# Weight sums of the 19 panel pairs: from VectorE into background transfers that add in device memory

## The reference, cut to what matters

```python
def _sq_relu_mlp(h, w1, w2):
    return jnp.square(jax.nn.relu(h @ w1)) @ w2
...
    h = _layer_norm_2(ALPHA * h + 0.5 * _swiglu(h, ffn2_w_gate[l], ffn2_w_up[l], ffn2_w_down[l]),
```

## Time and profile before

| | |
|---|---|
| median of 3 runs | 2706.53 us (2704.66 to 2708.64) |
| span of the profiled execution, first to last instruction | 2704.5 us |
| TensorE busy | 2652.7 us (98%) |
| VectorE busy | 1448.8 us (54%) |
| ScalarE busy | 1080.8 us (40%) |
| GpSimd busy | 279.4 us (10%) |
| DMA | 233 MB, 86 GB/s over the span |
| mean granted TensorE clock | 0.992 of full speed |

### The profile page before, as it was taken

One profiled execution on the slowest core, in us unless ns is written; L12 is line 12 of the kernel. 1 busy time (PEld: TensorE's weight loads), 2 busy tenths in 40 slices (PEclk: granted clock), 3 DMA queues, 4 the chain that ended last, 5 costly groups with the idle time before them and its releaser, 6 DMA issues.

```text
span 2704.5 us, 39939 instructions
## 1 busy us (share of the span) xinstructions
PE 2652.7 (98%) x16572; PEld 2343.7 (87%) x16572; DVE 1448.8 (54%) x2445; ACT 1080.8 (40%) x1743; POOL 279.4 (10%) x350
## 2 busy tenths in 40 slices
PE   8999999999999999999999999999999999999997
PEld 7888999999988888888888988888888897988887
DVE  5664665545543434576546543435666664645554
ACT  4655443323433233353234422323566543533333
POOL 1000300001200000210000300002211130300002
PEclk9999999999999999999999999999999999999998
DMA  4111223223111212222234232222322222222321
GB/s 143 55 48 48 79 94 127 86 79 126 55 63 63 97 62 85 86 86 94 76 104 141 85 113 97 86 94 71 110 86 71 70 87 79 66 98 82 106 88 61
DMA packets 67685, 232.98 MB, mean 86 GB/s; under 512 B 9008, under 2 KB 11440, under 8 KB 67120
## 3 DMA queue, kind: packets, MB, share of 16 engines
q1 hardware_dynamic: 67504, 230.41, 25.9%
HBM read 228.25 MB, written 2.10 MB: 85 GB/s over the span
## 4 chain that ended last, share of the span: by engine, by line
PE 88%; DVE 4%; ACT 3%; POOL 2%; issue 2%; DMA 1%; SPq 0%; DVEq 0%; POOLq 0%; ACTq 0%
PE ps L683 70%; PE ps L725 7%; PE ps L1030 2%; POOL R L3075 1%; PE ps L1161 1%; PE ps L733 1%; PE ps L925 1%; PE ps L885 1%; PE ps L1016 1%; POOL S L3060 1%; ACT HT L1450 1%; DVE R L2211 1%; DVE HT L2204 1%; DVE LENT L2162 1%; PE ps L1237 1%
## 5 line engine op out<-in xcount | busy, mean ns | idle before, releaser
L683 PE MATMUL ps<-XH,WH 128*128 128x264 f32 (+2 forms) x1552 | 470.5, 341 | 10.1 <-DVE XL L3034 7.6
L683 PE MATMUL ps<-XL,WH 128*128 128x264 f32 (+2 forms) x1552 | 457.1, 332 | 0.0
L683 PE MATMUL ps<-XH,WL 128*128 128x264 f32 (+2 forms) x1552 | 456.1, 332 | 0.0
L683 PE MATMUL ps<-HH,LENT 128*128 128x264 f32 (+2 forms) x2000 | 444.3, 318 | 3.0 <-DVE LENT L2162 1.9
L683 PE MATMUL ps<-XH,LENT 128*128 128x264 f32 (+2 forms) x1808 | 436.8, 332 | 5.0 <-DVE XL L2228 4.8
L2162 DVE TENSOR_TENSOR WL<-RAW,WH 128x1024 fp32r<-128x1024 f32 (+2 forms) x260 | 316.0, 1218 | 222.3 <-ACT WH L1406 221.0
L1406 ACT ACTIVATE WH<-RAW 128x1024 fp32r<-128x1024 f32 (+2 forms) x260 | 267.9, 1034 | 228.3 <-PE ps L683 187.6
L683 PEld LDWEIGHTS ps<-HH,LENT 128*128 128x128 f32 x2000 | 324.3, 189 | 31.6 <-DVE LENT L2162 2.3
L683 PEld LDWEIGHTS ps<-XH,LENT 128*128 128x128 f32 x1808 | 302.1, 189 | 42.5 <-DVE XL L2228 5.6
L2162 DVE TENSOR_TENSOR LENT<-RAW,LENT 128x1024 fp32r<-128x1024 f32 (+2 forms) x202 | 245.2, 1222 | 140.4 <-ACT LENT L1406 139.9
L683 PEld LDWEIGHTS ps<-XH,WH 128*128 128x128 f32 x1552 | 270.5, 190 | 50.0 <-issue 18.2
(11 more groups left out here) (256 smaller groups left out, 3395.4 us busy)
## 6 DMA issues: line engine op xcount, KB each, us to landing
RAW<-in_wf SPq DMA_DIRECT2D x128, 512.0 KB, 3.3
RAW<-in_wr SPq DMA_DIRECT2D x48, 512.0 KB, 3.3
RAW<-in_wg SPq DMA_DIRECT2D x44, 512.0 KB, 3.3
RAW<-in_wu SPq DMA_DIRECT2D x44, 512.0 KB, 3.3
RAW<-in_wd SPq DMA_DIRECT2D x32, 512.0 KB, 3.3
RAW<-in_we SPq DMA_DIRECT2D x24, 512.0 KB, 3.4
RAW<-in_wm SPq DMA_DIRECT2D x24, 512.0 KB, 3.2
RAW<-in_wro SPq DMA_DIRECT2D x16, 512.0 KB, 3.2
```

What stands on the lines that cost most here:

```text
L683: mm = e.matmul(o[:, to:to + m], wt, xt[:, k, c0 + a * m:c0 + (a + 1) * m], start=(n == 0 and j == 0), stop=(n == nk - 1 and j == 2))
```

## The change

The four sums of each pair are no longer made on VectorE. GpSimd issues, for seven groups of pairs (three for each MLP with two pairs each, one for the gates with seven), four copies from the weight matrix into a new array in device memory (`WSUM`) and then four transfers that add to what is there (`accum_op=ALU.add`): S1 = b2 + b1, S3 = a1 + b1, S2 = a1 + S1, S4 = a2 + S2. [...] Copies and adds are issued at fixed places of GpSimd's program: for the first MLP right after the constants, for the second after the first normalization (copies) and in the retention heads (adds), for the gates after `ln10` (copies), `ln11` (S1, S3), the memory normalization (S2) and `ln1` (S4). Each add waits for its copy, S2 and S4 also for the sum before.

SP loads by split, not by panel: `first` 512 KB, `22` 256 KB, `S13` and `S24` 512 KB each, the last two from `WSUM`, after the semaphores of their adds. A `RAW` buffer is free again once its one split is done. `S13` comes before `S24`, and `pair_steps` offers a split after each of the seven products. The new function `pair_up` has no pairs to work on here (no `wu` panel is in `PAIR_FIRST`).

```diff
-            if end:
-                s = ring.popleft()
...
+            s = ring.popleft()
+            ring.append(s)
+            units.append((kind, i, s, had.get(s)))
+            had[s] = (i, end)
...
-PAIR_UNITS = (("first", 2), ("22", 5), ("sums", 0), ("gap", 0), ("S24", 6), ("S13", 7))
+PAIR_UNITS = (("first", 2), ("22", 5), ("S13", 7), ("S24", 6))
...
-                if n in (1, 3, 5, 7):
-                    self.upto(i + 8, 1)
+                self.upto(i + 8, 1)
...
-        def weight_sums(i):
...
-                    e.tensor_tensor(b2, b2, acc(("pair", i, "A"), 1)[:, 0:n].unsqueeze(1).broadcast_to([P, 2, n]),
-                                    ALU.add).then_inc(*S.pair_add(i, "second"))
+                    e.scalar_tensor_tensor(b2, b2, -1.0, acc(("pair", i, "A"), 1)[:, 0:n].unsqueeze(1).broadcast_to([P, 2, n]),
+                                           ALU.mult, ALU.subtract).then_inc(*S.pair_add(i, "second"))
...
+        def sum_copies(key):
+
+            (name, first), n = key, SUM_PAIRS[key]
+            w4 = A[name][first:first + SUM_STEP[name] * n].rearrange("(q a) p (h k) c -> a h p q (k c)", a=SUM_STEP[name], h=2)
+            to = WSUM[key].rearrange("q p s c -> s p q c")
+            for m, (a, h) in {"S1": (1, 1), "S3": (0, 0), "S2": (0, 0), "S4": (0, 1)}.items():
+                e.dma_start(to[SUM_AT[m]], w4[a, h]).then_inc(*S.sum_copy(key, m))
+
+        def sum_add(key, m):
...
+            w.wait_ge(*S.sum_copy[key, m])
+            if m == "S2":
+                w.wait_ge(*S.sum_add[key, "S1"])
+            if m == "S4":
+                w.wait_ge(*S.sum_add[key, "S2"])
+            more = {"S1": w4[1, 0], "S3": w4[1, 0], "S2": to[SUM_AT["S1"]], "S4": to[SUM_AT["S2"]]}[m]
+            e.dma_start(to[SUM_AT[m]], more, accum_op=ALU.add).then_inc(*S.sum_add(key, m))
...
+        for key in ff_sums[0]:
+            sum_copies(key)
+        sum_adds(ff_sums[0], "S1", "S3", "S2", "S4")
         down_norm("ln00")
+        for key in ff_sums[1]:
+            sum_copies(key)
         down_norm("ln01")
         for h in range(4):
+            sum_adds(ff_sums[1], *(("S1", "S3"), ("S2",), ("S4",), ())[h])
...
         down_norm("ln10")
+        for key in gu_sums:
+            sum_copies(key)
         down_norm("ln11")
+        sum_adds(gu_sums, "S1", "S3")
...
+        sum_adds(gu_sums, "S2")
         down_norm("ln1")
+        sum_adds(gu_sums, "S4")
...
+            else:
+                key, q = SUM_OF[i]
+                for m in {"S13": ("S1", "S3"), "S24": ("S2", "S4")}[kind]:
+                    w.wait_ge(*S.sum_add[key, m])
+                a = SUM_AT[{"S13": "S3", "S24": "S2"}[kind]]
+                src = WSUM[key][q][:, a:a + 2, :].rearrange("p s n -> p (s n)")
+            if u >= NRAW:
+                w.wait_ge(*S.w_lo[u - NRAW])
+            e.dma_start(RAW[:, u % NRAW, 0:unit_cols(u)], src).then_inc(*S.raw_in(u))
```

More of the change, by code:

```diff
@@ L238, in lent_until @@
 def lent_until(name, idx, end=NSCR):
-    return max((i, 7 if i in PAIRS else 9) for _, i, s, _ in UNITS if i < AT[name, idx] and s and s[0] == "lent" and s[1] < end)
+    return max((i, 7 if i in PAIRS else 9) for _, i, s, _ in UNITS if i < AT[name, idx] and s[0] == "lent" and s[1] < end)
 class Signal:
@@ L1387, in split @@
             kind, i, place, before = UNITS[u]
[L1388 to L1401, removed]
+            raw, n = RAW[:, u % NRAW, :], unit_cols(u)
+            w.wait_ge(*S.raw_in[u])
             if before is not None:
@@ L1479, in relu2, with pair @@
             e.activation(HH[:, j, c0:c0 + T], TMP[:, j % 4, 0:T], ACT.Square).then_inc(*S.h_hi(stage, j, half))
-        def pair(i, rows, take):
+        def pair(i, tiles, take):
             stage = PAIRS[i]
             n = T_HALF[stage]
-            a, b = (TMP[:, r, :] for r in rows)
+            a, b = tiles
             to = {"11": (a, "A", 0), "S1": (b, "B", n), "S2": (a, "A", n), "22": (b, "D", 0)}
@@ L1501, in take @@
                 relu_free(i + 1, None)
-            pair(i, (idx % 4, idx % 4 + 1), take)
+            pair(i, [TMP[:, j % 4, :] for j in (idx, idx + 1)], take)
             for j in (idx, idx + 1):
@@ L1518, in pair_gate, with pair_up, take @@
                 e.activation(t, t, ACT.Silu).then_inc(*S.silu(i + n, None))
+        def pair_up(name, idx):
+            i, stage = AT[name, idx], f"gu{name[2]}c{idx // 8}"
+            def take():
+                if (name, idx - 2) in PAIR_FIRST:
+                    w.wait_ge(*S.up[AT[name, idx - 1], None])
+            pair(i, WIDE, take)
+            for j in (idx, idx + 1):
+                w.wait_ge(*S.up[AT[name, j], None])
+                w.wait_ge(*H_free(stage))
+                to_h(stage, j % 8, None, TMP[:, j % 4, 0:512], NM, 512)
         def t_hi(stage, q):
@@ L2271, in relu2, with pair @@
                             ALU.subtract).then_inc(*S.h_lo(stage, j, half))
-        def pair(i, rows, between=lambda: None):
+        def pair(i, tiles, between=lambda: None):
             stage = PAIRS[i]
             n = T_HALF[stage]
-            a, b = (TMP[:, r, 0:2 * n] for r in rows)
+            a, b = (t[:, 0:2 * n] for t in tiles)
             for at_end, m in enumerate(ah.pair_steps(i), 1):
@@ L2307, in pair_relu2, with pair_up, gated @@
                 to_h(stage, j % 8, None, two(TMP[:, j % 4, 0:T], T), c0, T)
+        def pair_up(name, idx):
+            i, stage = AT[name, idx], f"gu{name[2]}c{idx // 8}"
+            def gated(j, key):
+                t = TMP[:, j % 4, 0:512]
+                w.wait_ge(*S.pair_add[i, key])
+                w.wait_ge(*S.silu[AT[f"wg{name[2]}", j], None])
+                e.scalar_tensor_tensor(t, t, 0.5, WIDE[j - idx][:, 0:512], ALU.mult, ALU.mult).then_inc(*S.up(AT[name, j], None))
+            pair(i, WIDE, lambda: gated(idx, "12"))
+            gated(idx + 1, "second")
+            for j in (idx, idx + 1):
+                w.wait_ge(*S.up[AT[name, j], None])
+                to_h(stage, j % 8, None, TMP[:, j % 4, 0:512], NM, 512)
         def t_sum(stage, q):
@@ L3154, in sync, with weights @@
         w = Waits(e)
[L3156 removed]
+        def weights(u):
+            kind, i = UNITS[u][:2]
             name, idx, nk = PLAN[i]
[L3158 to L3160 removed]
+            if kind in ("plain", "first"):
+                src = A[name][idx].rearrange("p k n -> p (k n)")
+            elif kind == "22":
+                src = A[name][idx + 1][:, 4:8, :].rearrange("p k n -> p (k n)")
+            else:
+                key, q = SUM_OF[i]
[6 more added lines that the diff above has]
+            e.dma_start(RAW[:, u % NRAW, 0:unit_cols(u)], src).then_inc(*S.raw_in(u))
         done = [0]
         def weights_to(n):
[L3165 removed]
+            while done[0] < UNITS_TO[n]:
                 weights(done[0])
```

69 lines of the change are left out of this document (36 added, 33 removed).

## The result

The changed kernel takes 2731.28 us (median of 4 runs, 2723.24 to 2733.2) where the kernel before, run beside it, takes 2705.6: a ratio of 1.0087, 95% interval 1.0074 to 1.0100. That is 0.9% slower, some 26 us. The prediction had the sign (slower, chance 0.52), but only 6 us of it, and its range ended at 2721. The profiled execution has a span of 2731.3 us, 26.8 us more than the 2704.5 of before.

A forecast was written before the change was run, and what follows sets the result against it. It took TensorE as the bound, busy 2652.7 of 2704.5 us. Copies at the start (+4.5) and the clock (+1.5), all else 0, made +6: span 2710.5, plus 2.0 for the runs' median, 2712.5 us; range 2705 to 2721.

The forecast's parts named there:

- Background copies and adds in the middle: Transfers for the second MLP and gates: TensorE stays busy with panels split ahead, and SP's loads keep part of the engines; 0.
- Copies at the start: Twelve 512 KB copies from 9 us on delay the second panel and in_wfb on already full DMA engines; +4.5 us.
- the clock: After the longer TensorE gap at the start the granted clock may drop: 0 or 1.6 us, taken as +1.5.
- even share: At the start both queues split the time evenly: panel 5.0 us late, in_wfb lands at 29.0, L937 6.5 us late.
- The sums leave VectorE: In the pair stages, 52.4 us less VectorE work where TensorE hardly waits: 0 to -1.1 us, taken as 0.
- Signs: One addition per pair and half the activation sums become scalar_tensor_tensor, 686 against 687 ns: 0.
- SP loads by split: 38 more issues and 14.9 MB more loaded, DMA share about 0.32 in pair stretches: 0.
- Adds at the start: Twelve adds, some 35 to 90 us, at half a copy's rate by the skill page, with 300 us of room: 0.
- A: The copies' first data come after about 19 us, so idle DMA time hides them: 2703.5 to 2707.5 us; chance 0.23.
- B: At the start copies take much more than half, SP keeps 0.4, L937 is 11.5 us late: 2719.5 us; chance 0.14.
- C: First MLP's adds hold up SP's loads, or GpSimd's issuing delays the mixers: 2720 to 2760 us; chance 0.08.
- D: Freed VectorE matters more than its waits say, by over 5.4 us: 2700 us; chance 0.02.

The follow-up runs named there:

- e2: Changed kernel with the start's 24 transfers held until the attention is under way (issued from 84 us on): 2720.8 us, ratio 1.0051.
- e3: Changed kernel with the copies for the second MLP held to 435 us and those for the gates to 1265 us: 2714.43 us, ratio 1.0032.
- e4: Changed kernel with the delays of e2 and e3 together, all 56 transfers still made: 2705.04 us, ratio 0.9995.
- e8: Changed kernel with SP issuing the small tables in_lam and in_wfb ahead of the second and third panel: 2727.21 us, ratio 1.0072.
- e1: Changed kernel without its 56 background transfers; SP loads same-sized panels in place of sums, which are left out: 2704.56 us, ratio 0.9991.
- e7: As e4, but the start's transfers wait only until about 30 us, when SP has nothing to load: 2704.52 us, ratio 0.9990.
- e5: Kernel before with only the 28 copies added at the change's three places, results unused, no adds: 2731.02 us, ratio 1.0082.
- e11: As e4, but the second MLP's 12 copies are back at their place, each waiting for the one before: 2705.22 us, ratio 0.9996.

## Why the prediction was wrong, point by point

**The step that failed** is "Background copies and adds in the middle", put at 0 with the words "the loads of SP keep part of the engines". They do keep part, but a part was the wrong measure. The step reckoned with bandwidth (6.3 MB at 386 GB/s, 16 us) and with a stock of split panels. What happens is a matter of latency. A load issued beside the copies lands some 8 us later at 353 us (median 11.3 for 3.4) and some 5 us later near 1195 us (8.5 for 3.5). At 345 us, and again near 1195 us, a stage's space has just been given back, the three loads that SP issues are wanted at once, and ScalarE takes splits and activations in one fixed order, so that the lateness of a load goes over into the activations. That order is read from the traces; no run changed it. This term measures 14.7 us (e2), in place of 0. I had looked at the pair stretches, where TensorE has weights in stock (e3 and e4 show copies there to be free), and not at the microseconds in which the copies are issued; I had read "panels split ahead" from the wrong stage. In the trace of before ScalarE reaches a split of this very place 1.35 us before its panel has landed, so that no loaded panel lay in stock:

```profile
353.89 1.06 ACT L1406 ACTIVATE WH<-RAW 128x1024 fp32r<-128x1024 f32 x1 [1.35 <-DMA RAW<-in_wf]
```

**Copies at the start**, +4.5, and **the clock**, +1.5: the right kind of cause, too small. The late start of L948 is 7.4 us (6.5 for an even share, of which I took 4.5) and the clock 2.3 (I took 1.5); together 9.7 us in place of 6, and 8.3 us in the runs (e3). That the even share's landing of `in_wfb`, 29.0 us, is near the 29.9 seen was partly luck. From 11 to 23 us the copies hold 40% of the engines' time, not half, and the panel priced 5.0 us late is 1.5 late: its split starts at 15.50 us, its matmuls at 17.88 (16.42 before). The rest comes after that, when SP's queue has small packets. The two queues from 23 to 29 us (packets, MB, share of all engines):

```profile
q0 software_dynamic: 304, 1.11, 74.5%
q1 hardware_dynamic: 309, 0.49, 29.7%
```

As many packets each, and three quarters of the time for the copies. So L948 waits 5.95 us for the table, where the even share had it wait 1.5 us behind a later panel. With the tables ahead (e8) the panel is the late one.

The prediction weighed there a rule of the Trainium skill, page "DMA: Bandwidth & Descriptors", section "Queues, rings and completion order": the engines take turns between queues, packet by packet. Two loaded queues are now in the trace. The rows of 17 to 23 us:

```profile
q1 hardware_dynamic: 197, 1.12, 59.7%
q0 software_dynamic: 202, 0.72, 39.6%
```

and of 362 to 368 us:

```profile
q0 software_dynamic: 298, 1.08, 49.2%
q1 hardware_dynamic: 302, 1.11, 45.9%
```

By that rule the trace agrees, 197 to 202 and 298 to 302 (the page counts several descriptors to a packet; whether a packet of these rows is the same unit is not shown). My use of it was off: I had the copies' packets at 2 KB, their rows' size, and here they are 3.6 KB (1.08 MB in 298), close to SP's 3.7 (1.11 in 302). Turns between queues also do not tell how long a new load waits for its first turn. From 356 to 362 us, with SP's loads issued at 355.5 and 356.6, the counts are far from even:

```profile
q0 software_dynamic: 327, 1.21, 91.3%
q1 hardware_dynamic: 54, 0.22, 13.5%
```

**The sums leave VectorE**, 0 to -1.1: not contradicted (e1, e4, e7 stand between 0.9990 and 0.9995 of before, 1 to 2 us; a wait of 0.6 us is left of the 1.1). **Signs**, which differ because each transfer of the change adds: right, 687 ns each, as before. **SP loads by split**: right; the DMA share of the pair stretch is 0.35 for the 0.32 worked out, TensorE 215.00 of 215. **Adds at the start**: right, the last is issued at 81 us, and e5, without them, costs the same. The Trainium skill's page "Collectives: The Full Stack", section "The bandwidth ceiling: the fold count and why AG ≠ RS ≠ AR", would have them at half a copy's rate; here the same bytes take 1.7 times as long (49.4% against 28.8%), so that the trace agrees roughly.

**The rivals.** A (hidden start) is out: the copies show no packet before 11 us (I had them from 9) and take 39.5% of the engines' time from 11 to 17 us, well before the 19 us that it needed. B (a copy takes more than half) does not hold from 11 to 23 us (40%), but does from 23 to 29 (74.5%); its late start of 11.5 us stands against the 7.4 seen. C is out: among SP's waits there is none for an add, and 12 copies take GpSimd 8.4 us to issue. D is out by e1. No rival had copies in the middle delaying a load; the range, closed at 2721, reflects that.

## What to carry to other kernels

Price a background transfer by the landing time of a foreground load issued beside it (3.4 us became 11 here), at the microsecond where it is issued, and ask what is queued in program order behind the instruction that waits for that load; free engine time over a stage says nothing about that. Two cheap cures were shown: put the transfers where split weights are in stock (the loss of 26 us went to 0), or keep one small transfer in flight (the 512 KB copies at 353 us, free; over the whole kernel a quarter of the loss stayed). And freeing half-idle VectorE of 51 us was worth some 2 us at most, because in the pair stages TensorE had waited for it for one microsecond.

## What was not expected of the hardware

- A load's lateness does not grow with the number of copies issued: 9.8 to 11.9 us beside 4 copies of 512 KB, 6.2 to 12.8 beside 12, 3.5 to 7.3 beside one, 8.5 to 9.0 beside one of 1.8 MB. Twelve copies hold 6.3 MB, 20 us of transfer, and no load waited that long. So something bounds what stands before a load, near 7 to 8 us of copying. The expectation of e11 spoke of all copies issued before it; that is too simple. What sets the bound, and whether it is a backlog at all, stays open.
- Adds that hold the engines longer (49.4% against 28.8% for the same bytes) delay loads less (8.3 against 10.5 us). I can show that, and not why; each add's packets are about half the size (3264 for 6.29 MB against 1728), which may be part of it.
- A TensorE that has waited is slow afterwards. From 1220 to 1230 us it is busy for 5.81 of 10 us, and in the next 10 us it is busy all the time at a granted clock of 0.87. An estimate of what this costs: 2.3 us at the start, 2.2 at 353 us (9.1 us of new lateness less 6.9 idle) and 3.2 near 1200 us (7.4 less 4.2), 7.7 of the 26.8 us:

```profile
1220.00:1230.00 10.00, 5.81 (x18) 4.10 (x17) 9.29 (x11) 6.74 (x8) 0.00 (x0) 0.79 0.97 363
1230.00:1240.00 10.00, 10.00 (x39) 7.97 (x39) 4.55 (x5) 1.06 (x1) 0.00 (x0) 0.87 0.18 64
```
